# Gathers given a chunk each by a table, the gate stage three chunks later, and the second quad's weight parts made first

## The reference

```
h = rms_norm(x);  z = h @ w_in
x = x + concat(pool_mixer(z_pool), forgetting_attention(z_q, z_k, z_v, z_f)) @ w_out
h = rms_norm(x)
# PEER: 8 heads, product keys (2 x 128), the 16 best of 256 sums, 16384 experts
q = h @ w_query;  s1, s2 = q halves . sub_keys;  v1,i1 / v2,i2 = top_k(16)
top_s, pos = top_k(v1[:,None] + v2[None,:], 16);  idx = (i1*128 + i2)[pos];  g = softmax(top_s)
a = gelu(expert_u[idx] . h);  x = x + sum over (head, k) of g * a * expert_v[idx]
```

## Time and profile before

| | before |
|---|---|
| median of three runs | 1449.57 us |
| profiled execution | 1446.98 us, its span 1445.2 us |
| PE busy | 1407.3 us (97%) |
| DVE busy | 1111.8 us (77%) |
| POOL busy | 977.0 us (68%) |
| ACT busy | 629.4 us (44%) |
| granted TensorE clock, mean | 0.991 |
| HBM read | 351.57 MB, 273 GB/s over the span with the writes |

### The profile page before, as it was taken

How to read it: one execution, slowest core, us unless ns; L and a number is a source line. 1 busy time by engine, 2 the same in 40 slices (tenths; PEclk the granted TensorE clock), 3 DMA queues, 4 the chain that set the end, 5 groups by cost and what they waited for, 6 DMA issues and landing times.

```text
span 1445.2 us, 20837 instructions
## 1 busy us (share of the span) xinstructions
PE 1407.3 (97%) x7567; PEld 1248.0 (86%) x7567; DVE 1111.8 (77%) x1974; ACT 629.4 (44%) x1027; POOL 977.0 (68%) x560
## 2 busy tenths in 40 slices
PE   9999999997898999999999999999999999999998
PEld 7766788797898999999999999788888888888887
DVE  6678551799999896698898994677767777777775
ACT  5775462232232334566666664233333333333332
POOL 3421543275767888877777756578887888878883
PEclk9999999999999999999999999999999999999999
DMA  6321332276777799989999979997888888888883
GB/s 227 103 87 46 103 119 94 71 231 211 254 277 261 244 316 313 334 284 388 395 382 379 394 270 330 375 359 311 334 341 340 339 309 339 343 343 323 321 305 117
DMA packets 127291, 394.24 MB, mean 273 GB/s; under 512 B 12664, under 2 KB 29176, under 8 KB 127232
## 3 DMA queue, kind: packets, MB, share of 16 engines
q1 hardware_dynamic: 70384, 200.60, 38.8%
q0 software_dynamic: 41472, 151.01, 28.1%
q10 hardware_dynamic: 15376, 41.98, 7.4%
HBM read 351.57 MB, written 41.96 MB: 272 GB/s over the span
## 4 chain that ended last, share of the span: by engine, by line
PE 77%; DVE 18%; ACT 2%; issue 1%; DMA 1%; POOL 0%; DVEq 0%; SPq 0%; ACTq 0%
PE bank L817 22%; PE bank L818 22%; PE bank L819 22%; PE bank L1086 6%; DVE picked L1384 3%; DVE hit L1451 1%; DVE hit L1456 1%; DVE ku L1411 1%; DVE ku L1418 1%; DVE sc L1412 1%; DVE ab L1445 1%; DVE pos L1435 1%; DVE pos L1442 1%; DVE kv L1415 1%; DVE sel L1460 1%
## 5 line engine op out<-in xcount | busy, mean ns | idle before, releaser
L520 POOL TENSOR_TENSOR wl<-raw,wh 128x1024 fp32r<-128x1024 f32 x203 | 488.2, 2406 | 229.3 <-ACT wh L553 224.0
L817 PE MATMUL bank<-hh,wh 128*128 128x352 f32 (+1 forms) x1184 | 409.6, 346 | 23.1 <-POOL wl L520 22.6
L819 PE MATMUL bank<-hh,wl 128*128 128x352 f32 (+1 forms) x1184 | 397.7, 336 | 0.0
L818 PE MATMUL bank<-hl,wh 128*128 128x352 f32 (+1 forms) x1184 | 397.6, 336 | 0.0
L553 ACT ACTIVATE wh<-raw 128x1024 fp32r<-128x1024 f32 (+1 forms) x217 | 227.9, 1051 | 226.2 <-PE bank L819 140.5
L817 PE MATMUL bank<-wh,Wh 128*128 128x512 f32 x768 | 300.2, 391 | 3.5 <-DVE Wl L1570 3.5
L818 PE MATMUL bank<-wl,Wh 128*128 128x512 f32 x768 | 299.8, 390 | 0.0
L819 PE MATMUL bank<-wh,Wl 128*128 128x512 f32 x768 | 299.7, 390 | 0.0
L817 PEld LDWEIGHTS bank<-hh,wh 128*128 128x128 f32 x1184 | 225.3, 190 | 33.7 <-issue 20.1
L818 PEld LDWEIGHTS bank<-hl,wh 128*128 128x128 f32 x1184 | 226.1, 191 | 7.2 <-issue 0.2
L819 PEld LDWEIGHTS bank<-hh,wl 128*128 128x128 f32 x1184 | 224.8, 190 | 7.6
(11 more groups left out here) (217 smaller groups left out, 1681.4 us busy)
## 6 DMA issues: line engine op xcount, KB each, us to landing
raw<-uT_dram SPq DMA_DIRECT2D x128, 512.0 KB
xraw<-v_dram SPq DMA_DIRECT2D x72, 512.0 KB
raw<-v_dram SPq DMA_DIRECT2D x56, 512.0 KB
a_dram<-act_a ACTq DMA_DIRECT2D x64, 352.0 KB
wf<-a_dram SPq DMA_DIRECT2D x32, 704.0 KB, 6.5
raw<-wst_dram SPq DMA_DIRECT2D x40, 512.0 KB
gates_dram<-gbuf ACTq DMA_DIRECT2D x32, 512.0 KB
gt<-gates_dram SPq DMA_DIRECT2D x32, 512.0 KB
```

What stands on the lines that cost most here:

```text
L520: pool.tensor_tensor(wl[:, n % SPLIT, :], raw_of(n), wh[:, n % SPLIT, :].bitcast(F32), ALU.subtract).then_inc(w_lo, 1)
L817: pe.matmul(dst, ah, bh, start=start, stop=False)
L818: pe.matmul(dst, ah, bl, start=False, stop=False)
L819: return pe.matmul(dst, al, bh, start=False, stop=stop)
```

## The change

The gathers made before the gate stage come from a table, with the chunk behind whose split each stands; there are 62 instead of 65. The ups ahead of the gate stage are three more, those behind it three fewer. The dots made before the gate stage are 55 instead of 63 (46 + 9 instead of 52 + 11), those behind it 19 instead of 11 (11 beside three splits and 8 late, before 5 beside five splits and 6 late). ACT's three list and GELU steps and TensorE's UPS_FEW come later. The first quad's load is issued at the first chunk of v, four loads later. ACT makes quad 1's high parts ahead of its copy of v chunk 4, and VectorE makes quad 1's low parts ahead of the first row addition. GATE_DOTS, GATE_ROWS and the formula of the gate stage's gathers stay.

```diff
-           (2, 0): (2, 2, 3, 3), (2, 1): (3, 2, 3, 2)}
-UPS_RETR, UPS_SOFT, UPS_GATE = 60, 6, 48
+           (2, 0): (2, 2, 2, 2), (2, 1): (2, 2, 1, 1)}
+UPS_RETR, UPS_SOFT, UPS_GATE = 63, 6, 48
...
-UPS_FEW = 36
-MOVE_QUERY, MOVE_UP, FEW_GELU = 11, 8, 40
-ROWS_AT, ROWS_AGAIN = (-1, 4, 12), 41
-DOTS_RETR = FEW + 20
-DOTS_WAIT, DOTS_SOFT = 5, 11
+UPS_FEW = 43
+MOVE_QUERY, MOVE_UP, FEW_GELU = 14, 11, 47
+ROWS_AT = (0, 0, 1, 1, 2, 2, 3, 3, 6, 7, 8, 11, 12, 14, 15, 16, 17, 18, 19, 21, 22, 24, 25, 26, 27, 28, 29, 30, 32, 33,
+           35, 36, 37, 38, 39, 40, 42, 43, 45, 46, 48, 49, 50, 51, 53, 54, 55, 56, 57, 58, 59, 60, 61, 62, 65, 66, 66, 67, 67,
+           68, 68, 68)
+DOTS_RETR = FEW + 14
+DOTS_WAIT, DOTS_SOFT = 5, 9
 DOTS_GATE = DOTS_RETR + DOTS_SOFT
 GATE_DOTS, GATE_ROWS = 86, 86
-DOTS_LATE = 6
+DOTS_LATE = 8
...
-            first = FEW + ROWS + gate - ROWS_AGAIN
+            first = len(ROWS_AT)
             tail = DOTS - first - GATE_ROWS
...
-            retr = [j for j in range(first) if c == beside(j)]
+            retr = [j for j in range(first) if c == ROWS_AT[j]]
             gates = [first + i for i in range(GATE_ROWS) if c == gate + i * UPS_GATE // GATE_ROWS]
...
-                    if c == (-4, 3, 5)[q] if q < LOADS else c == QUAD * q - 6:
+                    if c == (0, 3, 5)[q] if q < LOADS else c == QUAD * q - 6:
...
             for q in range(1, QUADS):
-                hi_to(V_W + QUAD * q)
+                hi_to(V_W + QUAD * q - (q == 1))
                 weights_hi(q)
                 if q == 1:
+                    hi_to(V_W + QUAD)
...
                 split_lo(V_W + first + QUAD - 1)
+                if q == 1:
+                    weights_lo(q)
                 add_row(first)
...
-                if q < QUADS:
+                if 1 < q < QUADS:
                     weights_lo(q)
```

## The result

The kernel after takes 1496.76 us (median of 6 runs, 1495.01 to 1504.09) against 1448.9 us, a ratio of 1.0343 (95% interval 1.0318 to 1.0369). Forecast were 1483.6 us and a range of 1440 to 1518. The profiled execution has a span of 1493.8 us, 48.6 more than before.

A forecast was written before the change was run, and what follows sets the result against it. PE was taken as the bound, apart from waits mostly for GpSimd's splits. 1447.0 - 33.6 (query, retrieval) + 71.5 (gates) + 2.6 (tail) - 6.5 (second quad) = 1481.0 us, as a median 1483.6; range 1440 to 1518.

The forecast's parts named there:

- Query and retrieval: Before the gate stage: PE's waits for ACT's copies and GpSimd's splits shrink, -2.9 - 31.7 + 1.0 = -33.6 us.
- Gate stage: Gathers wait for dots, so splits, loads, ACT's copies and scalings come late for PE: +71.5 us.
- the turn: Gate stage, two chunks from one odd PE group to the next: 9.5 + L, 14.5 us, 3.25 us too long.
- L: Gate stage: time for a uT chunk's load to land, taken as 5.0 us, between 3.2 and 6.5.
- the ten chunks with one gather: Gate stage: their gather is released a group sooner, so two of 24 turns were given back.
- Rival C: Gate stage: PE's pauses bring the lower clock for half the stage, +97 us, 1581 us; chance 0.07.
- The rule for a landing: Gate stage loads: about 2.0 us plus bytes over 436,000 per us, an estimate of 3.2 us for 512 KB.
- Rival A: Gate stage: loads land fast, L near 3.2 us; 1444 us, to 1455 for L up to 3.7; chance 0.13.
- rival B: Gate stage: GpSimd's lead holds and the landing never stands in ACT's way; 1412 us; chance 0.12.
- the 2.1 us for the split of chunk 123: Tail: GpSimd's split stands behind the first gather of v, which waits for a late dot; +2.1 us (0 to 4).
- The cover given to load_quad(0): Tail: loading four chunks later costs nothing, as the gates' stores end before and DVE needs the data after three splits.
- Second quad: Quad 1's parts made earlier: PE's wait goes, 3.5 us, and 3.0 us lost at the lower clock, 6.5 us gained.

The follow-up runs named there:

- The lag alone in the kernel before: Kernel before with DOTS_SOFT 6 for 11 and nothing else, seven rows between gathers and dots in the gate stage instead of two: 1529.23 us, ratio 1.0574.
- the run with quartered loads: Kernel after with the loads of the 48 chunks beside the gate stage cut to a quarter of their columns: 1467.74 us, ratio 1.0143.
- DOTS_SOFT 14: Kernel after with five more dots ahead of the gate stage (14 for 9): 1420.07 us, ratio 0.9802.
- its tail put right: Kernel after with DOTS_SOFT 14, first eight gathers of expert_v a chunk later, DOTS_LATE 4 for 8, load_quad(0) two loads earlier: 1408.16 us, ratio 0.9734.
- one dot more: Kernel after with DOTS_SOFT 10 for 9: 1449.49 us, ratio 1.0013.

## Why the prediction was right, and where its sizes were off

*Query and retrieval.* Right to 1 us, with the gathers' waits down from 50.9 us in thirteen to 12.7 us in two: gather 53 waits for dot 45 as named, but 2.3 us and not 6, and gather 63, the second of the gate stage, waits 10.4 us for the first gate dot. One term did not come: UPS_FEW was to cost 1.0 us with PE waiting for dot 31, but VectorE still waits for PE's transposed rows, 2.0 us, and PE for nothing there.

*Gate stage.* The mechanism is the one predicted, step by step; the turn in the timeline has 9.55 + L. Between 600 and 925 us 49 gathers wait for dots, not 80 and more: about one a chunk, not two. The turns made 71.3 us where 71.5 were forecast, and that close a hit is in part luck, because three sizes differed: L was 4.65 us for 5.0; no turn is given back by the ten chunks with one gather (no two neighbouring chunks take less than 12.0 us, while before 46 of the 47 such pairs took 11.2 or 11.3); and the fixed part is 14.35 - 4.65 = 9.7 us for 9.5. The lag alone in the kernel before gives 14.35 - 4.57 = 9.8, the run with quartered loads 13.32 - 3.43 = 9.9. What the sum had at nothing is the entry into the stage: 8.5 us in the first two chunks, with the 10.4 us wait of gather 63, a wait of PE of 3.3 us for VectorE and one of 3.4 us for ACT's scalings. It is 3.0 us in the kernel before with the lag alone.

The lower level of the clock came with the waits, as this window of the kernel after, in and behind a wait of 3.9 us, shows:

```profile
700.00:706.90 6.90, 5.33 (x21) 5.34 (x22) 2.36 (x3) 3.91 (x9) 0.63 (x2) 0.52 0.69 233
```

How much of the loss is the clock's was not measured. Rival C, the lower level for half of the stage, did not come: 9 such stretches, 34 of 352 us. The turn does not follow them: it is 14.35 us as well in the kernel before with the lag alone, which has 17 us at the lower level.

*The rule for a landing.* The shortest loads in the gate stage took 3.1 us for 512 KB (of those whose landing is recorded in full) and 2.2 us for 128 KB. The Trainium skill, "DMA: Bandwidth & Descriptors", section "Anatomy of one DMA", gives 3.2 and 2.3 us as estimates from its formula (made for GpSimd's path). As a floor the traces agree; as the landing that a loop sees they do not: 4.65 and 3.43 us in the mean. Rival A, whose L is near that floor, was wrong for this reason; rival B was wrong because the landing did stand in ACT's way, 84.2 us of waits.

*Tail.* The term that failed is the 2.1 us for the split of chunk 123: the tail came out 7.1 us longer, with a wait of 5.3 us for that split and a stretch of 3.4 us at the lower clock behind it. The order was right (the split behind gathers 160 and 161, behind dot 153), but VectorE was late. These are its two late splits in the kernel after, and those of GpSimd beside them:

```profile
929.27 3.36 DVE L1535 TENSOR_TENSOR wl<-raw,wh 128x1024 fp32r<-128x1024 f32 x1 [1.38 <-ACT wh L544]
...
938.60 4.14 DVE L1535 TENSOR_TENSOR wl<-raw,wh 128x1024 fp32r<-128x1024 f32 x1 [0.83 <-ACT wh L544]
```
```profile
929.12 2.42 POOL L511 TENSOR_TENSOR wl<-raw,wh 128x1024 fp32r<-128x1024 f32 x1
...
939.23 2.42 POOL L511 TENSOR_TENSOR wl<-raw,wh 128x1024 fp32r<-128x1024 f32 x1
```

VectorE's take 3.36 and 4.14 us for 1.23 and end 1.1 us after GpSimd's end (931.54, 941.65); before, all 37 took 1.21 to 1.23 us. One of those ran beside a split of GpSimd as well, and there GpSimd's was the long one, 3.29 us for 2.4. The kernel before, VectorE and GpSimd:

```profile
866.57 1.22 DVE L1543 TENSOR_TENSOR wl<-raw,wh 128x1024 fp32r<-128x1024 f32 x1
```
```profile
866.75 3.29 POOL L520 TENSOR_TENSOR wl<-raw,wh 128x1024 fp32r<-128x1024 f32 x1 [6.51 <-ACT wh L553]
```

The Trainium skill, "SBUF — State Buffer", section "Who interferes with whom", says that an operation of VectorE with both inputs in SBUF contends with GpSimd's reads, that the ports they share are an exclusive lock, and of other modes of VectorE that whoever issues first has them for the whole instruction. The pair at 929 us and the one of the kernel before agree; in the pair at 939 us VectorE had begun earlier by the trace and was held all the same. Behind the second split VectorE pauses for 0.2 us in all up to the dot for which gather 160 waits, so up to 2.9 of the 5.3 us come from that split; this is read from the trace, no run took it away alone. Slow splits are not needed for such a wait: with DOTS_SOFT 14 the tail's three splits of VectorE take 1.22 or 1.23 us, and PE waits 6.2 us for the same split. There another thing made the dots late. The cover given to load_quad(0) was wrong as soon as the stage ran at speed: with DOTS_SOFT 14 VectorE waits for its data, ahead of the eight late dots:

```profile
871.11 1.23 DVE L1544 TENSOR_TENSOR wf<-gt,wf 128x1024 f32<-128x1024 f32 x1 [8.16 <-DMA wf<-a_dram]
```

*Residuals to quad 0.* 2.7 us for 0.5, inside its stated 0 to 3. The row of PE's waits is 2.4 us for the low parts of quad 0.

*Second quad.* Right to 0.1 us, alone and in the change.

## What to carry to other kernels

When two counters that move through a ring are shifted by different amounts, write down for each user of the ring which release it waits for, in items and then in time: here three rows fewer ahead and eight dots fewer made a distance of five dots, 2.8 chunks, the whole lead of the engine that issues them. A late producer need not be late itself to cost: ask what it triggers (here a load), who takes that in an in-order queue, and what of the critical engine's stands behind it. And try the one constant that restores the distance before judging the rest of a change: with it this one gained 2%, and with its tail put right 2.7%.

## What the runs showed of the hardware that was not expected

The landing of the same 512 KB load differs with how the stage runs: 4.65 us in the mean at 275 GB/s, 5.9 us at 321 GB/s with one dot more, 6.6 us at 348 GB/s with two. A loop that contains a transfer so gave back less than its fixed terms when it was shortened. It is not the traffic alone: at 352 GB/s in the kernel before and 359 GB/s with DOTS_SOFT 14, where no gather waits for a dot, the mean is 5.5 and 5.4 us. What makes that difference was not tested.

A split of VectorE beside one of GpSimd took up to 2.9 us more than alone, and in another pair GpSimd's took 0.9 us more.
